# Spreading a looped front over gather columns by TensorE columns moved instead of by step count

## The chip, the cores and the metric

One core of one Trainium2 chip runs the whole program. The metric is the device time of one execution in microseconds (us), median of the timed runs. The profile describes one profiled execution.

## The reference, cut to what matters

One layer of a hybrid trunk over 512 prompt tokens, 16 meta tokens and 32 sample tokens with a cache of 256. Mixers first, then PEER, a retrieval over 128 x 128 single-neuron experts:

```python
h = _rms(x, ln1_g)
cq, ckv, kpe, bq, bk, bv, iq, iw, ik, ga, gb = split(h @ w_in)
o_a = softmax(q . k + mask) @ v                      # MLA, 8 heads
sel = top_k(sum_h iw * relu(iq . ik), k_sel)         # index of mixer B
o_b = softmax(bq . bk[sel]) @ bv[sel]                # 8 heads
x = x + (sigmoid(ga) * (o_a @ w_o_a) + sigmoid(gb) * (o_b @ w_o_b)) @ w_out
t = _rms(x, ln2_g)
e, g = product_keys(t @ peer_wq, subkeys)            # 8 heads x 16 experts of each token
a = gelu(einsum('td,thkd->thk', t, u[e]))
x = x + einsum('thk,thkd->td', g * a, v[e])
```

Each token reads 128 rows of u and of v (1,024 floats each), so the kernel gathers 544 x 128 x 8 KB from HBM.

## The kernel before, in words

**Two kinds of work in one stream.** After a first stage (`project`) and a first front, the kernel (`stream`) walks through 544 *columns* b. A block is 32 queries and has SG = 32 columns; a column is one indirect gather of 128 rows of 8 KB (1.05 MB) issued by GpSimd into one of RING = 9 buffers `rows` (L1191). For each column VectorE makes the dot products with u (`dot`, L2349) and, every second column, the arguments of the gelu; ScalarE makes weights and a diagonal (`diagonals`, L1901 to L1910); TensorE applies v with eight small matmul instructions (`mix`, L1600), three columns later (LAG = 3). A gather into a buffer waits until `mix` has read it nine columns before.

**Fronts.** A front is everything ahead of the gathers for one prompt tile of 128 tokens: row projection with `w_row` (L1214), norms and rotations, 24 attention units of 2 ticks each (8 index, 8 MLA, 8 DSA), gates (L1420), `w_o` (L1435), `w_out` (L1449), `peer_wq` (L1470), key scores. Front p (p = 1, 2, 3) runs inside columns 128(p-1) to 128p-1. It is written as a generator `front(p)` for each of TensorE, ScalarE and VectorE; each `yield` is a *tick*, of which a looped front has 117, and each engine's program calls `next(ahead)` `ticks_at(b)` times in column b. So `ticks_at` alone sets, on all three engines in the same way, in which column each step stands. All engines run in order: a step that waits holds back the columns behind it.

**Ticks.** They are numbered k = -32 to 84. For k < 0 the code uses x = k + 28: x = 2 sum of squares of the new rows (L1951), x = 4 scale, x = 5 transposes, x = 7 to 13 projection (two 512 KB chunks of `w_row` a tick, 416 KB at 13), x = 10 and 12 latent sums and norm (L1974, L1983), x = 16 the up-projections with `w_uq` and `w_ukv`, x = 18 to 25 norms, gains and rotations on VectorE, x = 23 and 26 transposes of pairs and heads. From k = 0 a unit starts at every even k: scores on TensorE at k, `index_unit` at k + 2 or `logits` at k + 1 on VectorE, probabilities, transposes and values up to k + 6. The eight MLA units (k = 17 to 31 on VectorE) also carry `choose_some`: two rounds of max and replace over the score row, for the top 128 of mixer B. Gates stand at two of every six ticks of k = 0 to 47; turn 54, mix 56 to 63, out 65 to 68, norm 69 to 72, ask 73 to 80, key scores 82 and 83.

**Not moved by ticks.** In each block VectorE also selects the experts of the next block (`choose`, 11 parts at columns 2, 4, ... 22 of the block), and a `spread` of the next rows stands in column 31 of a block (L1580). SyncE loads weights in program order into a ring of WRING = 4 chunks (L1113), each as soon as its slot's last user on TensorE is done. The new rows `xb` are loaded (L1124) behind `pe` work of the same stream:

```python
def load_x(i):
    if i >= 2:
        sp.wait_ge(s_xc, first_block(i - 1))
```

`s_xc` counts `residual`, which TensorE runs at column 3 of a block, so the rows for fronts 2 and 3 are asked for at column 3 of the window of 128 columns in which they are used.

Of the kernel before, what the change touches and what calls it, by code (L numbers as in the profile page):

```python
# [10 lines left out]

# [12 lines left out]
P = 128  # L27
D = 1024
DC = D // P
SEQ, DEC, META, PAST = 512, 32, 16, 256  # L30
# [11 lines left out]
H = 8  # L42
# [24 lines left out]
PH = 8  # L67
TOPE = 16
SLOTS = PH * TOPE
# [616 lines left out]
U = 2  # L686
# [8 lines left out]
SETTLE = 4  # L695
START = SETTLE + 28
# [33 lines left out]
        self.base = START if p else 0  # L730


def ticks_at(b):

    p = b // SLOTS + 1
    if p >= NP:
        return 0
    n, k = Ticks(p).all + Ticks(p).base, b % SLOTS
    done = lambda k: n * min(k, SLOTS - 4) // (SLOTS - 4)
    return done(k + 1) - done(k)  # L740


# [80 lines left out]
def stream(nc, io, m, sem):  # L823
# [187 lines left out]
    with psum("ps_h", [P, D]) as ps_h, psum("ps_v", [P, QD]) as ps_v, \  # L1011
# [183 lines left out]
        def _(pe):  # L1195
# [411 lines left out]
            for b in range(NCOL + LAG):  # L1607
                if b % SLOTS == 0 and b // SLOTS + 1 < NP:
                    ahead = front(b // SLOTS + 1)
                if b >= LAG:  # L1610
                    if (b - LAG) % SG == 0:
                        residual((b - LAG) // SG)
                    mix(b - LAG)
                if b < NCOL:
                    for _ in range(ticks_at(b)):
                        next(ahead)
                    n = b // SG
                    if b % SG == SG - 1 and n + 1 < NB:
                        spread(n + 1)

        @block.scalar
        def _(act):
# [306 lines left out]
            for b in range(NCOL + LAG):  # L1929
                if b % SLOTS == 0 and b // SLOTS + 1 < NP:  # L1930
                    ahead = front(b // SLOTS + 1)
                if b >= SG and b % SG == LAG - 1:
                    block_out(b // SG - 1)
                if 2 <= b <= NCOL and b % 2 == 0:
                    diagonals(b - 2)
                if b < NCOL:
                    n = b // SG
                    for _ in range(ticks_at(b)):
                        next(ahead)
                    if n + 1 < NB and b % SG == 17:  # L1940
                        softmax(n + 1)

        @block.vector
        def _(dve):
# [428 lines left out]
            for b in range(NCOL + 1):  # L2373
                if b % SLOTS == 0 and b // SLOTS + 1 < NP:
                    ahead = front(b // SLOTS + 1)
                n, k = b // SG, b % SG
                if b < NCOL and k:
                    dot(b)
                if b >= 2 and b % 2 == 0:
                    arguments(b - 2)  # L2380
                if b < NCOL:
                    for _ in range(ticks_at(b)):
                        next(ahead)
                    if k == 0:
                        dot(b)
                    if n + 1 < NB and k % 2 == 0 and 1 <= k // 2 <= PARTS:
                        choose(n + 1, k // 2 - 1)
# [138 lines left out]
```

## Time and profile before

| | |
|---|---|
| device time, median of 3 runs | 1838.06 us (1835.85 to 1842.35) |
| span of the profiled execution | 1831.0 us |
| busy: PE, PEld, DVE, ACT, POOL | 69%, 38%, 71%, 32%, 29% |
| bytes moved | 696.47 MB, of them 570.53 MB by the gathers |
| windows of 128 columns, by their first dot product | 238.2, 628.6, 1026.6, 1428.2, 1748.7 us |

The trace gives the span from the first to the last instruction, and no other time of its own for that execution; the median of the runs is 7.1 us above this span. PE is TensorE's matmuls, PEld its weight loads, DVE VectorE, ACT ScalarE, POOL GpSimd, SP SyncE. Column c is the c-th L2349 instruction of the trace, counted from 0.

### The profile page before, as it was taken

What the parts mean: (1) busy time and instruction counts of PE and PEld (TensorE: products, weight loads), DVE (VectorE), ACT (ScalarE), POOL (GpSimd) and SP (SyncE); (2) the same over time, 40 slices, a digit from 0 to 9 for tenths busy, and PEclk for the clock granted to TensorE, in tenths of its full rate; (3) what the DMA queues carried; (4) which work ended last, traced back from release to release, by engine and by line L of the source; (5) the groups of instructions that cost most, each with busy time, mean ns of one, the idle gap of its engine ahead of it and who ended that gap; (6) DMA issues with size and microseconds to landing.
All of it is one profiled execution on the core that took longest, in us unless ns stands there. A gap on an engine that the chain in (4) does not pass through costs nothing.

```text
span 1831.0 us, 26290 instructions
## 1 busy us (share of the span) xinstructions
PE 1256.7 (69%) x8990; PEld 693.1 (38%) x8990; DVE 1307.8 (71%) x3842; ACT 580.0 (32%) x2009; POOL 522.6 (29%) x569
## 2 busy tenths in 40 slices
PE   8989746678778565788877485889878543434353
PEld 3666612344444222455445132556536111111111
DVE  5561495888766577898767667898757768686754
ACT  2331223424323233334422333334423222222222
POOL 0100032333322323332323322322323333333332
PEclk9999859778798778788898587887997555555555
DMA  6325499999999999999999999998999999999997
GB/s 263 94 99 174 149 426 408 403 425 425 421 424 421 422 421 401 396 425 398 424 423 421 425 382 404 424 413 330 421 423 419 425 427 426 426 426 426 426 422 306
DMA packets 119380, 696.47 MB, mean 380 GB/s; under 512 B 17983, under 2 KB 21118, under 8 KB 49102
## 3 DMA queue, kind: packets, MB, share of 16 engines
q0 software_dynamic: 78848, 570.53, 74.7%
q1 hardware_dynamic: 36686, 121.83, 17.6%
q10 hardware_dynamic: 3712, 2.43, 0.4%
q8 instruction: 71, 1.16, 0.2%
q14 instruction: 63, 0.52, 0.1%
HBM read 691.65 MB, written 3.02 MB: 379 GB/s over the span
## 4 chain that ended last, share of the span: by engine, by line
DMA 37%; PE 27%; DVE 22%; issue 5%; ACT 4%; POOL 1%; ACTq 0%; DVEq 0%; POOLq 0%
DMA rows<-in_peer_uv,index 28%; DVE rows L2349 9%; PE ps_v L1600 6%; PE ps_f L1420 4%; PE ps_f L1470 3%; PE ps_f L1449 3%; DMA wch<-in_w_row 3%; PE ps_f L1214 3%; DMA wch<-in_w_out 2%; PE ps_h L1580 2%; DMA wch<-in_peer_wq 2%; PE ps_f L1435 1%; DVE score L2074 1%; DMA wch<-in_w_ukv 1%; PE ps_f L1298 1%
## 5 line engine op out<-in xcount | busy, mean ns | idle before, releaser
L1191 POOL DMA_INDIRECT rows<-in_peer_uv,index x544 | 512.7, 943 | 1211.4 <-PE ps_v L1600 1010.4
L2349 DVE CUSTOM_DVE_ANT_0 rows<-rows,ps_h 128x1024 f32<-128x1024 f32 x544 | 657.5, 1220 | 271.7 <-DMA rows<-in_peer_uv,index 228.7
L1600 PE MATMUL ps_v<-rows,diag 128*32 128x256 f32 x4352 | 434.2, 515 | 462.4 <-ACT diag L1910 462.1
L1600 PEld LDWEIGHTS ps_v<-rows,diag 128*32 128x32 f32 x4352 | 125.9, 133 | 719.2 <-ACT diag L1910 612.2
L1901 ACT ACTIVATE tan<-arg 128x2 f32<-128x2 f32 x272 | 55.4, 204 | 784.4 <-DVE arg L2359 765.4
L1904 ACT ACTIVATE weight<-tan,lead 128x1 f32<-128x1 f32 x544 | 180.8, 379 | 9.1
L1910 ACT ACTIVATE diag<-sel,weight 128x32 f32<-128x32 f32 x544 | 140.7, 305 | 0.0
L1420 PEld LDWEIGHTS ps_f<-bufh,wch 128*128 128x128 f32 x768 | 114.4, 233 | 22.0 <-issue 19.6
L1420 PE MATMUL ps_f<-bufh,wch 128*128 128x128 f32 x768 | 121.3, 323 | 0.0
L1214 PE MATMUL ps_f<-wch,bufh 128*128 128x512 f32 (+1 forms) x192 | 80.4, 559 | 18.3 <-DMA wch<-in_w_row 18.0
L1449 PE MATMUL ps_f<-wch,bufb 128*128 128x512 f32 x96 | 53.1, 693 | 18.4 <-DMA wch<-in_w_out 18.4
L1470 PE MATMUL ps_f<-bufh,wch 128*128 128x128 f32 x384 | 54.9, 302 | 10.8 <-DMA wch<-in_peer_wq 10.8
L1470 PEld LDWEIGHTS ps_f<-bufh,wch 128*128 128x128 f32 x384 | 50.4, 212 | 22.3 <-issue 16.5
L1214 PEld LDWEIGHTS ps_f<-wch,bufh 128*128 128x128 f32 x192 | 32.9, 202 | 60.6 <-issue 33.2
L1580 PE MATMUL ps_h<-hrows,rep 32*128 32x512 f32 x68 | 51.7, 898 | 3.0 <-DVE dots L2349 3.0
L2358 DVE TENSOR_TENSOR lead<-dots,halfw 128x2 f32<-128x2 f32 x272 | 43.9, 161 | 9.4
L1435 PE MATMUL ps_f<-bufq,wch 128*128 128x128 f32 x384 | 49.2, 281 | 0.8 <-DMA wch<-in_w_o 0.4
L1435 PEld LDWEIGHTS ps_f<-bufq,wch 128*128 128x128 f32 x384 | 44.7, 191 | 11.0 <-issue 9.2
L2349 DVE DVE_READ_ACCUMULATOR2_ANT dots<- 128x1 f32 x544 | 44.8, 82 | 0.0
L1715 ACT COPY probT<-ps_f 128x128 f32<-128x128 f32 (+3 forms) x64 | 26.5, 413 | 56.4 <-PE ps_f L1310 56.4
L2356 DVE SCALAR_TENSOR_TENSOR cube<-dots 128x2 f32<-128x2 f32 x272 | 42.7, 157 | 0.6
L2359 DVE SCALAR_TENSOR_TENSOR arg<-cube,dots 128x2 f32<-128x2 f32 x272 | 42.0, 154 | 0.0
(359 smaller groups left out, 1675.8 us busy)
## 6 DMA issues: line engine op xcount, KB each, us to landing
wch<-in_w_gate SPq DMA_DIRECT2D x60, 512.0 KB, 8.1
wch<-in_w_row SPq DMA_DIRECT2D x36, 512.0 KB, 11.3
wch<-in_w_o SPq DMA_DIRECT2D x32, 512.0 KB, 7.8
wch<-in_w_out SPq DMA_DIRECT2D x32, 512.0 KB, 10.1
wch<-in_peer_wq SPq DMA_DIRECT2D x32, 512.0 KB, 10.6
rows<-in_peer_uv,index POOLq DMA_INDIRECT x544, 13.8
w_tok<-in_w_tok SPq DMA_DIRECT2D x4, 1640.0 KB, 13.7
wch<-in_w_uq SPq DMA_DIRECT2D x6, 384.0 KB, 4.9
```

Of the source, the lines that this page charges most:

```text
L1191: pool.indirect_dma_start(rows[c % RING][:, :, :].rearrange("p a d -> p (a d)"), None, io.peer_uv[:, :], at).then_inc(s_uv[c % RING], 16)
L1214: ins = nc.tensor.matmul(ps_f[:, 2 + c % 2, 0:cols], buf_h[:, k, :], w[:, b, :], start=(k == 0), stop=(k == DC - 1))
L1420: ins = nc.tensor.matmul(gated(p)[:, a, :], w[:, k, :], h_of(p)[:, k, 0:n], start=(k == 0), stop=(k == DC - 1))
L1435: ins = nc.tensor.matmul(blended(p, j)[:, x, :], w[:, x, k, :], ot_of(p)[:, x, k, 0:n], start=(k == 0), stop=(k == 3))
L1449: ins = nc.tensor.matmul(ps_f[:, c, :], mt_of(p)[:, k, at_of(i)], w[:, 512 * c:512 * (c + 1)], start=(k == 0), stop=(k == DC - 1))
L1470: ins = nc.tensor.matmul(ps_f[:, 2 + n % 2, 0:x], w[:, k, :], h_of(p)[:, k, 0:x], start=(k == 0), stop=(k == DC - 1))
L1580: ins = nc.tensor.matmul(ps_h[:, 512 * j:512 * (j + 1)], rep[here, :, :].rearrange("p a m -> p (a m)"), hrows[i % 2][here, 512 * j:512 * ( ...
L1600: ins = nc.tensor.matmul(ps_v[GROUP * a:GROUP * (a + 1), :], diag[:, c % DRING, :], rows[c % RING][:, 1, QD * a:QD * (a + 1)], start=False ...
L1901: nc.scalar.activation(tan[:, s:s + 2], arg[:, s:s + 2], ACT.Tanh, scale=TANH).then_inc(s_tan, 1)
L1904: nc.scalar.activation(weight[:, s + j:s + j + 1], tan[:, s + j:s + j + 1], ACT.Identity, scale=lead[:, s + j:s + j + 1], bias=lead[:, s + ...
L1910: nc.scalar.activation(diag[:, (c + j) % DRING, :], sel[:, :], ACT.Copy, scale=weight[:, s + j:s + j + 1]).then_inc(s_diag, 1)
L2349: v.tensor_tensor_reduce(out=u, in0=u, in1=ps_h[:, :], scale=1.0, scalar=0.0, op0=ALU.mult, op1=ALU.add, accum_out=dots[:, c % KEEP:c % KE ...
```

## The change

`ticks_at` spreads the 117 ticks over the first 124 columns of the window. Before, tick t (0 to 116) stands where `117 * k // 124` passes it, so about one tick a column. After, each tick has a weight, the TensorE columns that it moves (`moved`), plus LIGHT = 320; ticks are cut at equal shares of the running sum. Nothing else changes: the same instructions, waits and loads on each engine, in the same order within each front and within each engine's column work.

```diff
+def moved(p):
+    at, nk = Ticks(p), META + P * p + P
+    tile_blocks = p + 1
+    due = lambda k, lag, low: k >= lag and (k - lag) % U == 0 and low <= (k - lag) // U < at.units
+    cols = []
+    for k in range(-at.base, at.all):
+        x = k + START - SETTLE
+        n = 0
+        if k < 0:
+            n += {5: 8 * 160, 8: 7 * 160, 13: 3 * 160, 16: 8 * 320, 23: 9 * 160, 26: 16 * 160}.get(x, 0)
+            if 7 <= x < 14:
+                n += 4 * 512 if x < 13 else 8 * 160
+            n = max(n, {2: 720, 4: 720, 6: 700, 10: 700, 12: 800, 16: 900, 18: 900, 19: 700, 21: 1000, 22: 1200, 23: 900,
+                        24: 900, 25: 600}.get(x, 0))
+        if due(k, 0, 0):
+            n += nk
+        if due(k, 3, H):
+            n += (tile_blocks + 1) * 160
+        if due(k, 5, H):
+            n += tile_blocks * 160
+        if 0 <= k < 6 * DC and k % 6 in (2, 4):
+            n += 8 * 160
+        if k == at.turn or k == at.rows or k == at.res:
+            n += 8 * 160
+        if at.mix <= k < at.mix + DC or at.ask <= k < at.ask + PH:
+            n += 8 * 160
+        if at.out <= k < at.out + 4:
+            n += 4 * 512
+        if k in (at.key, at.key + 1):
+            n += 8 * 160
+        cols.append(n + LIGHT)
+    return cols
+
+LIGHT = 320
+
 def ticks_at(b):
-    p = b // SLOTS + 1
+    p, k = b // SLOTS + 1, b % SLOTS
     if p >= NP:
         return 0
-    n, k = Ticks(p).all + Ticks(p).base, b % SLOTS
-    done = lambda k: n * min(k, SLOTS - 4) // (SLOTS - 4)
+    cols = moved(p)
+    ends = list(itertools.accumulate(cols))
+    done = lambda k: sum(e * (SLOTS - 4) <= ends[-1] * min(k, SLOTS - 4) for e in ends)
     return done(k + 1) - done(k)
```

## Rows read from the trace of the kernel before

**Rows 1.** The page: GB/s moved in 40 equal slices of the span

```profile
GB/s 263 94 99 174 149 426 408 403 425 425 421 424 421 422 421 401 396 425 398 424 423 421 425 382 404 424 413 330 421 423 419 425 427 426 426 426 426 426 422 306
```

**Rows 2.** Busy time by stretch: fronts 1, 2, 3 and the window without front

```profile
core 0: us, PE busy (x) PEld busy (x) DVE busy (x) ACT busy (x) POOL busy (x), PEclk, DMA share, GB/s
225.50:628.60 403.10, 281.26 (x2037) 156.28 (x2040) 304.63 (x921) 134.63 (x466) 126.70 (x134) 0.80 1.01 417
628.60:1026.60 398.00, 289.57 (x2108) 160.44 (x2109) 301.82 (x876) 138.12 (x464) 121.28 (x128) 0.83 1.01 415
1026.60:1428.20 401.60, 311.12 (x2204) 182.68 (x2208) 309.45 (x876) 142.63 (x464) 120.57 (x128) 0.81 0.99 404
1428.20:1748.70 320.50, 141.78 (x1076) 43.26 (x1080) 240.12 (x708) 84.62 (x328) 119.83 (x128) 0.51 1.01 426
```

**Rows 3.** The same view, shorter stretches in which GB/s falls

```profile
281.00:341.20 60.20, 37.77 (x210) 15.86 (x212) 38.76 (x100) 20.89 (x62) 16.06 (x17) 0.77 1.01 412
341.20:374.60 33.40, 25.77 (x207) 15.82 (x207) 29.39 (x93) 11.90 (x41) 12.74 (x14) 0.85 0.99 397
675.50:735.50 60.00, 36.66 (x211) 15.05 (x213) 38.61 (x100) 20.89 (x62) 16.24 (x17) 0.84 1.00 404
735.50:773.20 37.70, 30.97 (x231) 17.70 (x230) 33.81 (x106) 14.48 (x48) 14.38 (x15) 0.80 0.98 390
839.10:881.20 42.10, 38.53 (x279) 23.96 (x278) 36.92 (x121) 19.39 (x73) 13.26 (x14) 0.87 1.00 395
1074.40:1134.40 60.00, 37.27 (x200) 15.56 (x203) 38.71 (x100) 20.90 (x62) 15.12 (x16) 0.79 0.98 391
1134.40:1174.30 39.90, 34.56 (x252) 21.19 (x252) 36.49 (x109) 15.12 (x48) 15.22 (x17) 0.80 0.98 400
1174.30:1228.20 53.90, 43.22 (x290) 29.14 (x294) 49.88 (x127) 18.80 (x67) 15.18 (x16) 0.81 1.01 419
1228.20:1280.90 52.70, 48.90 (x329) 33.03 (x327) 44.39 (x131) 20.44 (x72) 14.06 (x15) 0.81 0.88 339
```

**Rows 4.** Waits, 1060 to 1135 us: total, times, longest

```profile
ACT sg L1633 <- PE ps_f L1214: 19.3, 3, 13.0
...
DVE pst L1983 <- ACT pst L1644: 9.3, 1, 9.3
...
DVE rel L1999 <- ACT oab L1656: 5.4, 1, 5.4
```

**Rows 5.** TensorE in order of time during the third front's projection

```profile
1061.29 3.70 PE L1214 MATMUL ps_f<-wch,bufh 128*128 128x512 f32 x8
...
1074.16 1.98 PE L1214 MATMUL ps_f<-wch,bufh 128*128 128x512 f32 x4 [1.17 <-DMA wch<-in_w_row]
1079.20 3.78 PE L1214 MATMUL ps_f<-wch,bufh 128*128 128x512 f32 x4 [3.06 <-DMA wch<-in_w_row]
```

**Rows 6.** VectorE in order of time, column 310 to 312

```profile
1187.33 0.70 DVE L2094 CUSTOM_DVE_ANT_0 logit<-ps_f,biasA 128x528 f32<-128x528 f32 x1
...
1191.05 0.69 DVE L2298 TENSOR_TENSOR cand<-posf,num 128x512 f32<-128x512 f32 x1
...
1193.23 1.22 DVE L2349 CUSTOM_DVE_ANT_0 rows<-rows,ps_h 128x1024 f32<-128x1024 f32 x1
...
1195.85 0.19 DVE L2303 SCALAR_TENSOR_TENSOR index<-pick 128x32 uint32<-128x32 f32 x1
```

**Rows 7.** The page's DMA issues: count, KB, median us to landing

```profile
wch<-in_w_row SPq DMA_DIRECT2D x36, 512.0 KB, 11.3
...
rows<-in_peer_uv,index POOLq DMA_INDIRECT x544, 13.8
```

**Rows 8.** The new rows of front 2: issue on SP

```profile
632.44 0.33 SPq L1124 DMA_DIRECT2D xb<-in_x_prompt  x1
```

**Rows 9.** VectorE around it: columns 130 and the first sum

```profile
630.86 1.22 DVE L2349 CUSTOM_DVE_ANT_0 rows<-rows,ps_h 128x1024 f32<-128x1024 f32 x1
...
647.37 1.22 DVE L1951 CUSTOM_DVE_ANT_0 oab<-xb 128x1024 f32<-128x1024 f32 x1
```

**Rows 10.** The view of tile xb: issue to landing

```profile
DMA to landing us min/median/max: 7.2/8.3/8.7
```

More of the change, by code:

```diff
@@ L15 @@
+import itertools
 import numpy as np
```

## The prediction

> **What bounds the kernel now.** I read the slices first. From the sixth slice on the DMA engines move 419 to 427 GB/s, except in a few slices at 330 to 413 [rows 1]: the loop over gather columns is bound by DMA, and what is left to gain are the dips. The window without a front takes 320.5 us for 128 columns, 2.50 us a column, at 426 GB/s with VectorE 75% and TensorE 44% busy [rows 2]. So a faster engine is worth nothing as such; time is won only where the transfers run dry.
>
> How much is that? Stretches with a front that do not dip run at 419 to 425 GB/s [rows 1, 3]; I take 421 as their ceiling, my choice. Idle time is then stretch x (1 - GB/s / 421): 403.1 us at 417 gives 3.8 us, 398.0 at 415 gives 5.7, 401.6 at 404 gives 16.2 [rows 2], in all 25.7 us. This is the most that any spreading of the steps can win.
>
> The shorter stretches say where [rows 3]. *Projection and heads*, x = 7 to 27 (columns 18 to about 45 of a window): 1.3 + 1.9 us in front 1, 2.4 + 2.8 in front 2, 4.3 + 2.0 in front 3, together 14.7. *Attention*: 2.6 us in front 2 (839 to 881), 10.3 in front 3 (1228 to 1281: 52.7 x 82/421), together 12.9. The two sums make 27.6, two more than the windows, since other stretches lie above 421.
>
> The waits tell why the first kind dips. In front 3 ScalarE waits up to 13.0 us for the second projection group, VectorE behind it 9.3 us for the root of the latents (L1983), and later 5.4 us for the up-projection [rows 4]. Behind VectorE stand the dot products, behind those `mix`, behind that the gathers. The cause is the load: a 512 KB chunk lands 11.3 us after its issue [rows 7], its slot is freed two ticks before it is needed, and before the change two ticks are two columns, some 5 us.
>
> The second kind is work. A unit with `choose_some` in front 3 takes VectorE 3.72 us (1187.33 to 1191.05), a column with its arguments 1.31 us (1193.23 to 1195.85, two columns), a part 8 or 9 of `choose` 2.18 us (1191.05 to 1193.23) [rows 6]. From 1193.23 (column 311) to 1228.2 (column 320) nine columns take 35.0 us [rows 3, 6], where DMA needs 9 x 2.50 plus two gate chunks at 1.25 (0.524 MB at 421 GB/s), 25.0 us. The gathers absorbed about 10 us of lag before GB/s fell: that is the slack of the ring, and I use it below.
>
> **The change, part by part.** It removes and adds no instruction. I worked out the new columns from `moved`: the weights sum to 142,768, 150,960 and 159,152, thus 1,151 to 1,283 a column.
>
> *Projection* (x = 7 to 13, weight 2,368 each, 3,488 at 8) stood in columns 12 to 19. It now stands in 8 to 21 (front 1), 7 to 19, 7 to 18: 1.8 to 2.1 columns a tick. SP's chunk loads move with their users. From freeing to need there are now four columns at 2.50 us plus four chunks at 1.25 us, 15 us, against 11.3 us to landing [rows 7]. The waits of 9.3 and 5.4 us go [rows 4]. From column 18 to 32 VectorE is busy 38.7 of 60 us [rows 3]; with the 9.3 and 5.4 us of waits gone it needs 45, and DMA needs 14 x 2.50 plus some eight chunks, 45. So DMA should hardly idle. Short waits stay: the up-projection (x = 16) and its copy (x = 17) fall into one column in all three fronts, and norms of 1 to 3 us follow densely. I leave 1.4 us of idle for each front: 14.7 - 4.2 = 10.5 us won. Bounds: 0 (the waits return elsewhere) and 14.7.
>
> *Index units and choose_some* (k = 0 to 31) stood in columns 34 to 67. They stand in 32 to 63 in front 3, and not evenly: k = 0 to 18 shrinks from 20 columns to 14. `moved` counts TensorE's columns, not VectorE's work. The heavy units k = 17 to 31 move from columns 52 to 67 to 45 to 63; before, they began as `choose` ended (columns 34 to 54), now they share 45 to 54 with its parts 6 to 10. A part costs 1.65 us in the mean: without a front VectorE is busy 240.1 us, 128 x 1.31 of them for columns, 72 for 44 parts [rows 2, 6]. VectorE in columns 45 to 63: 19 x 1.31 + 8 x 3.72 + 5 x 1.65 + 2 (final selection and last index unit, three passes over the score row, each like L2094's 0.70 [rows 6]) = 65 us. DMA: 19 x 2.50 + 5 gate chunks = 53.7. Lag grows by 11.5 us. With up to 3 us brought along and 10 of slack, 1.5 to 4.5 us are lost; if the slack is only 7, up to 7.5.
>
> *Units k = 28 to 47* stood in 20 columns of front 3 (64 to 84) and get 24 (60 to 84). TensorE is busy 48.9 of 52.7 us there [rows 3], and its work per column falls by a sixth, to about 2.5 to 2.9 us, DMA's own pace. The tail of the dip goes. So front 3's attention loses 6 us after against 10.3, a gain of 4.3 (bounds: 10.3, and a loss of 4 if there is no slack at all). In front 2 rows of 400 keys cost less; 2.6 becomes 1.5, a gain of 1.1. Front 1 has no dip there and gets none.
>
> *The new rows.* Empty ticks x = -4 to 1 took columns 1 to 6; x = 2 stood in column 7 and now stands in column 2. VectorE finishes column 130 at about 632.3, and the load of `xb` is issued at 632.44 [rows 8, 9], 15 us ahead of its use at 647.37 before. It lands after 8.3 us [rows 10], so VectorE now stands still until about 641, in fronts 2 and 3. Behind it stand the dot products from column 131, ScalarE at its root, and `mix` from column 130; up to seven issued gathers, 17 us of transfers, are outstanding. The first gather that waits for the late `mix` follows at about 649, before they end. I charge 1 us a front, 2 in all (bounds 0 and 4 each).
>
> *Ticks that now share a column* (for instance k = 51 to 53, where TensorE needs ScalarE's copy and VectorE the result) wait for each other at close range. VectorE is under 60% loaded there, so the ring hides most; 2 us, bounds 0 and 6. The steps from 56 on move by at most seven columns, in stretches at 419 to 425 GB/s [rows 1]: nothing.
>
> Sum: -10.5 - 4.3 - 1.1 + 2 + 2 = -11.9 us. The profiled span of 1831.0 becomes 1819.1; the median of the runs, 7.1 us above the span, becomes 1826.2.
>
> **A rule against it.** In the rows a chunk after a wait of 1.17 us runs in 1.98 us, after one of 3.06 us in 3.78 us, at the lower clock level [rows 5]. Spreading leaves more gaps, but each holds a `mix`: of 6.8 us per projection tick TensorE works about 5. The Trainium skill (TensorE: Matmul & The Clock Gate, Loop structure matters more than you think) asks for matmuls back to back, and calls a long DMA wait between them the bad case, since the array goes cold. By that the sum would be the third rival's; by the row with the short wait it is mine.
>
> **Rivals.** *Idle time only moves* (0.22). Front 3's overload of VectorE comes ten columns earlier, and what the projection wins is lost in columns 40 to 63 and at column 2. For it: the same 310 us of VectorE work [rows 2]. Against it: the waits of 9.3 and 5.4 us are not work [rows 4]. Time: -5 to +5, about 1838.
>
> *Pile-up on VectorE: slower* (0.10). The slack is spent at column 40 by the heads. Then lag turns into idle time in full: 14.5 us in front 3 (+4 against 10.3), about 7 in front 2 (+4.5), 4 in front 1 (+4), and the projection wins only half, 5: with +2 and +2, about +11, 1849. It decides when more than some 8 of 10 us of slack are gone at column 40. Against it: after the heads the ring refilled, since GB/s is back at 419 from 1174 [rows 3].
>
> *A cold projection: slower* (0.08). At 3.78 us a chunk, 12.8 chunks, 13 columns of `mix` at 1.08 and 1.8 for the gains take TensorE 64 us against 48.5 for DMA: 15.5 less 10 of slack is 5.5 us lost a front, over 4.9 now. Instead of winning 10.5 it costs 2: +0.6, and +5 if half of the slack is used, 1843. It decides above about 3.3 us a chunk.
>
> The forecast, a gain of more than 0.3%, has 0.58; 0.02 is left for other losses.
>
> **Numbers.** A difference under 0.3% (5.5 us) can't be told from none. Faster 0.58, same 0.22, slower 0.20. The low end is 1816: nearly 22 of the 25.7 us. The high end, 1844, takes in the moved idle time and the cold projection and part of the pile-up. The forecast's own range is 1816 to 1832.
>
> **What would show it.** Right: no 9 us wait of L1983 on L1644; 415 GB/s or more through projection and heads; the third window under 396 us. A new wait of L1951 for the load of `xb` of 7 to 9 us in fronts 2 and 3. VectorE above 95% busy from column 45 to 63 of front 3, with the dip there, earlier and shallower. Wrong: that dip deeper than 10 us, GB/s falling near column 10 of windows 2 and 3, or L1214 chunks mostly at 3.7 us.

## The result: 0.64% slower

The changed kernel takes 1846.98 us in the median of 6 runs (1845.93 to 1850.64), the kernel before 1836.95 us in 6 runs (1830.6 to 1842.35). The ratio is 1.0064, with a 95% interval of 1.0043 to 1.0085, so it is slower by 12 us (the two medians are 10.0 us apart) where the forecast was 12 us faster. The profiled span went from 1831.0 to 1844.1 us.

First the slices of the page after, against [rows 1]: the GB/s moved.

```profile
GB/s 261 95 98 173 155 425 422 417 425 424 425 424 422 422 349 423 421 387 398 425 423 422 392 400 395 412 331 366 424 422 424 426 426 426 425 426 424 427 420 304
```

Some dips are gone (408 and 403 in slices 7 and 8, 401 and 396 in slices 16 and 17 [rows 1]), and new ones stand beside them (349 in slice 15, 392 to 400 in slices 23 to 25), while the deepest has doubled its width (331, 366). Busy time by stretch, for the three windows with a front and the one without, against [rows 2]:

```profile
core 0: us, PE busy (x) PEld busy (x) DVE busy (x) ACT busy (x) POOL busy (x), PEclk, DMA share, GB/s
225.50:628.10 402.60, 285.04 (x2039) 159.94 (x2041) 305.73 (x922) 135.65 (x467) 127.21 (x134) 0.79 1.01 420
628.10:1030.30 402.20, 292.21 (x2109) 164.93 (x2112) 301.45 (x876) 137.94 (x464) 121.26 (x128) 0.82 0.99 407
1030.30:1441.40 411.10, 305.19 (x2204) 181.79 (x2208) 309.56 (x876) 142.24 (x464) 121.37 (x128) 0.81 0.98 396
1441.40:1762.00 320.60, 141.32 (x1076) 43.32 (x1080) 240.13 (x709) 84.61 (x328) 119.82 (x128) 0.51 1.01 426
```

The engines' busy times are those of before to within three per cent, and the last window is the same to 0.1 us. The difference is time in which DMA has nothing to move. By the prediction's measure, stretch x (1 - GB/s / 421), this idle time is 1.0, 13.4 and 24.4 us in the three windows, against 3.8, 5.7 and 16.2: front 1 wins 2.8, front 2 loses 7.7, front 3 loses 8.2, together 13.1 us, the 13 us of the span. Only the sum is firm: the windows themselves got 0.5 us shorter, 4.2 and 9.5 us longer, since a gather can be moved early, in the window ahead of its column. Shorter stretches of fronts 2 and 3 say where. They are cut at columns 0, 18 and 32, and for front 3 also at 45, 64 and 88:

```profile
628.10:683.90 55.80, 34.95 (x203) 14.62 (x202) 40.09 (x129) 18.38 (x52) 16.07 (x17) 0.75 0.91 360
683.90:736.40 52.50, 30.64 (x180) 13.55 (x184) 38.68 (x101) 17.51 (x57) 14.52 (x15) 0.75 1.02 423
1030.30:1086.90 56.60, 35.52 (x194) 14.57 (x194) 40.67 (x131) 18.51 (x52) 15.06 (x16) 0.72 0.95 379
1086.90:1143.30 56.40, 32.89 (x204) 15.20 (x208) 37.84 (x97) 19.76 (x61) 15.38 (x16) 0.76 1.02 422
1143.30:1176.60 33.30, 28.45 (x215) 18.88 (x216) 31.09 (x92) 12.96 (x41) 11.69 (x12) 0.87 0.96 386
1176.60:1246.10 69.50, 51.12 (x365) 32.96 (x363) 63.61 (x161) 21.20 (x75) 18.95 (x21) 0.79 0.92 354
1246.10:1314.00 67.90, 58.48 (x433) 39.81 (x433) 54.38 (x165) 28.83 (x102) 22.49 (x24) 0.85 0.97 384
```

Three things are to be seen. Columns 18 to 32, at 404 and 391 GB/s before [rows 3], are full at 423 and 422. Columns 0 to 18, full before (424 and 425 GB/s), are at 360 and 379: 8.1 and 5.6 us idle. And columns 45 to 64 of front 3 take 69.5 us at 354 GB/s, 11.1 us idle.

The waits in 1060 to 1145 us, against [rows 4]:

```profile
ACT sg L1674 <- PE ps_f L1255: 15.4, 3, 6.5
...
DVE rel L2040 <- ACT oab L1697: 6.9, 1, 6.9
```

ScalarE's longest wait for a projection group fell from 13.0 to 6.5 us, and VectorE's 9.3 us for the root of the latents (L1983 on L1644) is gone. The wait for the up-projection (L1999 on L1656 before) is still there, and grew from 5.4 to 6.9 us.

**Columns 0 to 18.** The waits in 626 to 665 us (total, times, longest):

```profile
PE ps_f L1241 <- DVE qh L2001: 10.3, 1, 10.3
DVE oab L1992 <- DMA xb<-in_x_prompt: 8.4, 1, 8.4
```

L1992 is L1951 of before, the sum of squares of the new rows. It waits 8.4 us for the load, as forecast. What follows in GpSimd's, TensorE's and DMA's time is in these rows, first the gather issues:

```profile
636.48 0.94 POOL L1232 DMA_INDIRECT rows<-in_peer_uv,index  x1 [0.30 <-issue]
649.76 0.94 POOL L1232 DMA_INDIRECT rows<-in_peer_uv,index  x1 [12.35 <-PE ps_v L1641]
655.28 0.94 POOL L1232 DMA_INDIRECT rows<-in_peer_uv,index  x1 [3.35 <-PE ps_v L1641]
661.68 1.09 POOL L1232 DMA_INDIRECT rows<-in_peer_uv,index  x1 [5.46 <-PE ps_v L1641]
```

then TensorE's first projection tick,

```profile
654.91 5.89 PE L1255 MATMUL ps_f<-wch,bufh 128*128 128x512 f32 x8
```

and busy time in steps of 4 us:

```profile
644.00:648.00 4.00, 1.97 (x8) 1.57 (x8) 3.86 (x14) 0.75 (x3) 0.00 (x0) 0.50 0.73 309
648.00:652.00 4.00, 1.93 (x16) 0.59 (x16) 3.90 (x9) 0.54 (x3) 1.87 (x2) 0.50 0.27 57
652.00:656.00 4.00, 2.10 (x10) 0.77 (x11) 3.83 (x16) 1.29 (x5) 0.71 (x1) 0.50 0.90 360
656.00:660.00 4.00, 4.00 (x7) 1.67 (x6) 3.83 (x16) 1.29 (x5) 0.22 (x1) 0.58 0.99 372
660.00:664.00 4.00, 4.00 (x31) 1.55 (x30) 3.93 (x9) 1.29 (x5) 2.02 (x2) 1.00 0.88 288
664.00:668.00 4.00, 4.00 (x27) 2.48 (x29) 3.83 (x14) 1.76 (x6) 0.95 (x2) 1.00 0.89 323
```

The next gather is issued at 649.76; the prediction said "about 649". But the transfers under way ended at about 647, not after 649, so DMA stands almost still from 648 to 652 (57 GB/s). Then VectorE is busy 3.8 of every 4 us and TensorE, at the low clock level (0.50), needs 5.89 us for two chunks. The ring has little in reserve, so a second dip follows from 660 to 668: at 656 us 1.5 gathers are issued and not yet moved, at 662 us 1.0. (This is counted from the trace: the gathers that GpSimd has issued, less what their queue has moved at 1.049 MB each.)

The low level isn't new, though. In the kernel before, the first projection tick of this front and a step of 4 us ahead of it read:

```profile
659.01 5.24 PE L1214 MATMUL ps_f<-wch,bufh 128*128 128x512 f32 x8
```

```profile
656.00:660.00 4.00, 3.22 (x19) 1.10 (x18) 3.96 (x6) 1.22 (x5) 1.22 (x2) 0.50 1.02 432
```

There too the granted clock is 0.50 and the tick is slow, and DMA stays full at 432 GB/s. What differs is the reserve when it comes: 3.4 gathers issued and not yet moved at 656 us, and not 1.5.

### The profile page after: what moved, and what is told of

Its sections match the earlier page's. It is cut to its first block, busy times and chain, and to the rows that moved or that the text cites. A ratio compares the mean times of both kernels' runs of the same rounds, so it can differ in the third digit from the quotient of the medians.

```text
span 1844.1 us, 26278 instructions
## 1 busy us (share of the span) xinstructions
PE 1255.8 (68%) x8990; PEld 700.4 (38%) x8990; DVE 1308.2 (71%) x3842; ACT 579.9 (31%) x2009; POOL 523.8 (28%) x569
## 4 chain that ended last, share of the span: by engine, by line
DMA 34%; PE 27%; DVE 24%; issue 5%; ACT 3%; POOL 1%; ACTq 1%; DVEq 0%; POOLq 0%
DMA rows<-in_peer_uv,index 26%; DVE rows L2390 9%; PE ps_v L1641 6%; DMA wch<-in_w_row 4%; PE ps_f L1461 3%; PE ps_f L1476 3%; PE ps_f L1490 2%; PE ps_h L1621 2%; PE ps_f L1511 2%; PE ps_f L1255 2%; DVE score L2115 2%; DVE best L2114 2%; DMA wch<-in_w_out 1%; POOL rows L1232 1%; ACT diag L1951 1%
## 5 line engine op out<-in xcount | busy, mean ns | idle before, releaser
L1641 PE MATMUL ps_v<-rows,diag 128*32 128x256 f32 x4352 | 426.7, 509 | 458.1 <-ACT diag L1951 457.7
L1951 ACT ACTIVATE diag<-sel,weight 128x32 f32<-128x32 f32 x544 | 141.1, 306 | 1.8 <-PE ps_v L1641 1.7
L1476 PE MATMUL ps_f<-bufq,wch 128*128 128x128 f32 x384 | 58.0, 313 | 0.9 <-ACT bufq L1805 0.9
L1476 PEld LDWEIGHTS ps_f<-bufq,wch 128*128 128x128 f32 x384 | 53.1, 222 | 12.4 <-issue 8.2
L1339 PE MATMUL ps_f<-bik,bufb 64*128 64x144 f32 (+2 forms) x96 | 38.5, 488 | 1.7 <-ACT kt L1726 1.0
## 6 DMA issues: line engine op xcount, KB each, us to landing
wch<-in_peer_wq SPq DMA_DIRECT2D x32, 512.0 KB, 10.1
```

Of the source, the lines that this page charges most:

```text
L1476: ins = nc.tensor.matmul(blended(p, j)[:, x, :], w[:, x, k, :], ot_of(p)[:, x, k, 0:n], start=(k == 0), stop=(k == 3))
L1641: ins = nc.tensor.matmul(ps_v[GROUP * a:GROUP * (a + 1), :], diag[:, c % DRING, :], rows[c % RING][:, 1, QD * a:QD * (a + 1)], start=False ...
L1951: nc.scalar.activation(diag[:, (c + j) % DRING, :], sel[:, :], ACT.Copy, scale=weight[:, s + j:s + j + 1]).then_inc(s_diag, 1)
```

## The experiments

Each is the kernel before or after with another column for some ticks, but for the two that leave work out. A ratio is to the kernel before in the same rounds and is known to about 0.2%, so a difference of two ratios is known to some 0.25 to 0.3%, about 5 us. `was(p, t)` is the column of tick t before, `now(p, t)` after, `START` = 32 is the tick k = 0. Theory A has two separate prices, the early wait for the rows and VectorE's overload in the attention, and a gain from the projection. B puts all of the loss in the attention, C all in the early wait.

**Only the first nine ticks early.**

```diff
+def column(p, t):
+    return now(p, t) if t < 9 else was(p, t)
```

> The kernel before, with only the first nine ticks of each looped front (x = -4 to 4: four ticks' worth of nothing, the sum of squares of the new rows, its root, the scaling) in the columns in which the change puts them, x = 2 in column 2 instead of 7. Everything from x = 5 on stands as before. Theory A (the early wait for the new rows runs the ring dry): 6 to 13 us slower than before, a wait of 8 to 9 us of the sum of squares for the load of xb in fronts 2 and 3, GB/s well under 400 in the 20 us behind it. Theory B (the loss is the pile-up of VectorE work in the attention, and the ring absorbs the early wait): under 2 us slower, GB/s over 410 there.

Measured: 1846.74 us, ratio 1.0055 (1.0033 to 1.0077), 10 us slower. Waits in front 2, and columns 0 to 18 of both fronts:

```profile
DVE oab L2013 <- DMA xb<-in_x_prompt: 7.8, 1, 7.8
```

```profile
628.00:677.00 49.00, 26.60 (x171) 11.13 (x170) 39.67 (x127) 15.03 (x47) 14.05 (x15) 0.69 0.96 391
1034.00:1083.20 49.20, 27.08 (x172) 11.38 (x169) 39.63 (x127) 15.03 (x47) 14.04 (x15) 0.69 0.97 395
```

Nine ticks with about 2 us of VectorE's work cost nearly as much as the whole change. B, in which the ring absorbs the wait, is out. The wait is 7.8 us, a little under the 8 to 9 expected. Only 6.5 us of idle time stand at the spot; with the projection still in column 12, the second dip of the change is missing. The rest is spread over later stretches of this profile (384 GB/s in columns 64 to 88 of front 2, 344 in front 3), where lag meets dips that are there anyway. How it divides between places in other runs, one profile can't say.

**TensorE's transposes early too.** The same with `t < 10`.

> As the run with only ticks x = -4 to 4 early, and in addition x = 5, TensorE's transposes of the scaled rows, in column 5 or 4 as in the change, so that TensorE too waits for the late rows and holds back its mix instructions. If TensorE's wait adds to the price: 3 to 8 us slower than that run, 13 to 18 slower than before. If VectorE's wait is all of it (my expectation, as mix for column 130 can't run earlier in any case): within 3 us of that run.

Measured: 1845.76 us, 1.0043 (1.0023 to 1.0062). By this run the early rows cost 8 us. No more than the run above: TensorE's wait of 9.3 us adds nothing measurable to VectorE's.

**Only the attention moved.**

```diff
+def column(p, t):
+    return max(now(p, t), 33) if START <= t < START + 54 else was(p, t)
```

> The kernel before, with only ticks k = 0 to 53 (index, MLA and DSA units and gates) in the columns in which the change puts them; k = 17 in column 49, 47, 45 instead of 52. Projection, heads and everything from k = 54 on stand as before. Theory A (both places cost): 4 to 9 us slower than before, of it 1 to 3 in front 2 and 3 to 6 in front 3, the dip of front 3 beginning some seven columns earlier. Theory B (all of the loss is here): 10 to 14 us slower. Theory C (the deeper dip in the attention is only lag brought along from the early wait): within 2 us of before.

Measured: 1849.49 us, 1.0054 (1.0033 to 1.0075), some 10 us slower, a little above what A gave it and at the lower end of B's. Columns 48 to 64 and 64 to 88 of front 3:

```profile
1194.40:1248.20 53.80, 41.62 (x294) 27.80 (x294) 49.60 (x125) 18.83 (x67) 14.23 (x16) 0.81 0.87 323
1248.20:1316.30 68.10, 58.70 (x433) 39.70 (x433) 54.48 (x167) 28.93 (x102) 22.77 (x24) 0.85 0.97 384
```

53.8 x 98/421 = 12.5 us idle, as in the change, though there was no wait for new rows. C is out: the dip is made on the spot. Front 2 of this profile lost more than A's 1 to 3 us: 12.5 us idle over its window, against 5.7 before.

**The change without its attention.**

```diff
+def column(p, t):
+    return now(p, t) if t < START else max(was(p, t), now(p, START - 1))
```

> Ticks x = -4 to 27 as in the change (new rows in column 2, projection spread over 7 to 21), everything from k = 0 on in the columns of before. So the change without its attention. The early rows alone cost about 10 us, the attention alone about 10, the whole change about 10; if these add up, spreading the projection wins about 10, and this kernel is within 3 us of before, idle time in columns 0 to 18 as in the change (8.1 and 5.6 us in fronts 2 and 3), none in 18 to 32. If the spread projection wins nothing: 8 to 12 us slower than before.

Measured: 1840.85 us, 1.0032 (1.0018 to 1.0046). 6 us slower, outside the 3 I gave, and short of the 8 to 12 for no gain at all. Against the run with nine early ticks (1.0055) the projection's gain is 4 us, against the one with ten (1.0043), which moves x = 5 as this one does, 2 us, and neither is clear of the noise of a difference. Idle time is 7.3 and 4.3 us in columns 0 to 18, and -0.2 and 0.8 in 18 to 32.

**The rows late again.** Empty ticks weigh more, so x = 2 stands in column 6 or 7 and k = 17 in 52, 50, 48.

```diff
-        cols.append(n + LIGHT)
+        cols.append(n + (1280 if x < 2 else LIGHT))
```

> The changed kernel with a weight of 1,280 instead of 320 for the six empty ticks, so that x = 2 stands in column 6 or 7 again; the projection still has 11 to 13 columns (11 to 25), and k = 17 stands in column 52, 50, 48. Theory A: no wait of L1992 for xb above 1 us; 9 to 15 us faster than the changed kernel, so 0 to 5 us faster than before. Theory B: 0 to 3 us faster than the changed kernel, so 7 to 10 us slower than before.

> x_late once more beside the two others and the kernel before on the same chip, to place the projection's gain in the same rounds: between the change with its rows late and the hand-fitted run. Spread projection and late rows with the change's own attention: 2 to 6 us faster than before.

Measured twice: 1834.54 us, 0.9977 (0.996 to 0.9994), and 1833.44 us, 0.998 (0.9965 to 0.9995). No wait for `xb` is left in either profile. Against the changed kernel's ratio of 1.0064 this is 0.85% or 16 us, a little more than the 9 to 15 expected. One constant turns the change from a loss into a small gain. Not all of it is the wait, since the heavy units moved by three columns too.

**Late rows and equal attention.** In addition to the edit above:

```diff
+    a = at.base
+    cols[a:a + at.turn] = [sum(cols[a:a + at.turn]) // at.turn] * at.turn
```

> As x_late, and in addition ticks k = 0 to 53 share their columns equally, so that k = 17 stands in column 53 or 54 and k = 31 in 67, as before. Left of the change are the spread projection and the last third. Theory A: 8 to 14 us faster than before; the dips of the attention as before or smaller, those of projection and heads gone. Theory C: the same as x_late within 2 us. If the spread projection won nothing: within 2 us of before.

Measured: 1832.86 us, 0.9975 (0.9953 to 0.9998), 1828 to 1841 in 12 runs. A had asked for 8 to 14 us, and got 4.5. The time is the one that C gave, the same as with the rows late alone (0.9975 against 0.9977), though C itself was out already. Columns 48 to 64 of front 3 are nearly full (1.2 us idle), but 64 to 88 lose 16.7 us in the profiled execution. That one took 1840.89 us and belongs to four of the twelve at 1840 to 1841; the other eight took 1828 to 1835, and none of them was profiled. Equal spacing gives TensorE's dense units back the few columns of before. In this one profile the dip moved on.

**The rounds left out,** in both kernels:

```diff
             def choose_some(i, h):
                 q, nk = queries(i), keys(i)
+                if i >= 2:
+                    return
```

> The changed kernel without the max and replace rounds of choose_some in the looped fronts (the top 128 of mixer B isn't selected there), 3 us of VectorE work less in each of eight units a front; all else stays. If the idle time in columns 48 to 64 (3.6 us in front 2, 11.1 in front 3) is VectorE's overload: it falls to under 1 us in both, and the kernel is 10 to 18 us faster than the changed one, so 0 to 8 us faster than before; what stays is the early wait for the rows. If it is something else that moved with the ticks (TensorE, waits between engines that now share a column): less than 5 us faster than the changed kernel.

> The kernel before without the same rounds. If the idle time in columns 64 to 88 of front 3 (10.6 us) is lag that the rounds in columns 52 to 67 leave behind: it falls to under 4 us, and the kernel is 7 to 12 us faster than before. If it is TensorE's own density there (48.9 of 52.7 us busy): it stays above 6 us, and the kernel is under 5 us faster.

Measured: 1826.84 us after, 0.9944 (0.9925 to 0.9964), and 1825.17 us before, 0.9925 (0.9899 to 0.9951). Columns 45 to 64 of front 3 after:

```profile
1171.30:1227.70 56.40, 49.29 (x364) 32.87 (x367) 40.42 (x113) 24.04 (x84) 18.79 (x20) 0.86 1.01 425
```

With 23 us of VectorE work fewer (40.4 against 63.6) the stretch is full, at the same spacing and the same TensorE work: the idle time there was VectorE's. Taking the work away wins 1.2% or 22 us after, where 10 to 18 were expected, and 14 us before, where 7 to 12 were. The two kernels no longer differ measurably. In before, the idle time of columns 64 to 88 falls from 10.6 to 3.9 us: most of that dip, which I had in part laid to TensorE, was lag from the rounds.

**A placement by hand for both engines.** On top of x_late:

```python
def column(p, t):
    at = Ticks(p)
    k, c = t - at.base, now(p, t)
    for lo, hi, a, b in ((0, 16, now(p, at.base), 51), (17, 31, 52, 66), (32, 47, 67, 88), (48, 53, 89, 90)):
        if lo <= k <= hi:
            c = a + (b - a) * (k - lo) // (hi - lo)
    return c if k < 54 else max(c, 90)
```

> As x_late (rows late, projection spread), but with the attention fitted to both engines by hand: index units one tick a column up to column 51, the heavy units k = 17 to 31 in 52 to 66 between two choose sweeps of VectorE, and k = 32 to 47, TensorE's dense part, over 67 to 88 instead of 66 to 84 or so. If places of both engines decide: idle time of columns 48 to 88 of front 3 under 8 us, 2 to 6 us faster than x_late, so 6 to 11 faster than before. If the dip of 64 to 88 comes whatever the spacing: within 2 us of x_late.

> The hand-fitted run once more, beside fit_att and x_late on the same chip: 10 to 15 us faster than before, and by the projection's gain faster than fit_att.

Measured: 1824.25 us, 0.9927 (0.9904 to 0.995), and in other rounds 1828.14 us, 0.9955 (0.994 to 0.997): 8 to 13 us faster than before, the best of all with the full work done. The first was a little better than the 6 to 11 us expected, the second missed the low end of its 10 to 15. Front 3, columns 0 to 18, 18 to 32, 48 to 64, 64 to 88:

```profile
1027.90:1075.30 47.40, 31.43 (x198) 13.03 (x198) 40.06 (x129) 15.04 (x48) 15.42 (x16) 0.68 1.01 425
1075.30:1132.50 57.20, 34.14 (x188) 14.38 (x188) 38.56 (x100) 20.89 (x61) 15.64 (x16) 0.86 1.02 421
...
1172.10:1228.70 56.60, 45.74 (x323) 31.97 (x324) 53.49 (x134) 21.13 (x73) 15.98 (x17) 0.85 1.00 408
1228.70:1295.10 66.40, 59.95 (x446) 39.66 (x445) 58.26 (x172) 27.73 (x96) 22.00 (x24) 0.85 0.94 368
```

Idle 1.7 + 8.4 = 10.1 us in columns 48 to 88, not under 8, and hardly less than the 10.9 of before; what front 3 wins stands in columns 18 to 32 (4.3 us before, none here).

**The same attention with the old projection.** `was(p, t)` in place of `now(p, t)`, k = 0 in column 34, and the steps from k = 54 on in the columns of before.

> Projection and heads as before, ticks k = 0 to 53 as in the hand-fitted run. It splits that run's gain of 13 us. If most of it is the spread projection: 0 to 6 us faster than before, with idle time in columns 18 to 32 as before (1.3, 2.4, 4.3 us). If most of it is the attention: 8 to 13 us faster than before.

Measured: 1832.57 us, 0.9988 (0.9968 to 1.0008), so 0 to 6 us faster as for "mostly the projection", with 1.7, 2.9 and 2.7 us idle in columns 18 to 32. In the same rounds the hand placement is at 0.9955: spreading the projection, with the rows late, is worth 0.33%, 6 us, give or take 5. The two also differ in the steps from k = 54 on, by a few columns.

Idle us in fronts 2 / 3, from one profile of each of seven kernels, by the measure above (slightly negative where GB/s is above 421), cut at these columns:

| | 0-18 | 18-32 | 32-48 | 48-64 | 64-88 |
|---|---|---|---|---|---|
| before | -0.4 / -0.5 | 2.4 / 4.3 | 2.6 / 2.0 | -0.5 / 0.3 | 2.4 / 10.6 |
| after | 8.1 / 5.6 | -0.2 / -0.1 | 0.0 / 2.7 | 3.6 / 11.1 | 2.2 / 6.0 |
| rows early | 3.5 / 3.0 | 1.2 / 1.0 | 4.8 / 4.4 | -0.5 / 0.3 | 6.5 / 13.3 |
| attention only | -0.3 / -0.5 | 2.6 / 2.7 | 4.5 / 1.5 | 1.3 / 12.5 | 5.5 / 6.0 |
| x_late | 0.0 / -0.4 | -0.3 / 0.0 | 2.9 / 1.3 | 2.4 / 6.8 | 4.5 / 3.7 |
| after, no rounds | 7.8 / 6.0 | -0.2 / 0.3 | -0.3 / 4.0 | -0.4 / -0.4 | -0.2 / 0.5 |
| fit | -0.3 / -0.5 | -0.3 / 0.0 | 1.0 / 1.2 | -0.2 / 1.7 | 5.7 / 8.4 |

## Why the prediction was wrong

The frame held: the loop is bound by DMA, the windows' idle time accounts for the difference of the spans, and each of the places named moved. Two terms had the wrong size, and with them the sum the wrong sign. By the table, fronts 2 and 3 win 8.9 us in columns 18 to 48 and lose 14.6 in 0 to 18 and 10.1 in 48 to 88; front 1 wins 2.8.

- **The new rows** were charged 2 us. The wait (8.4 and 8.9 us) and the time of the next gather (649.76) were forecast nearly to the microsecond. The failing step is "I charge 1 us a front". It rested on "up to seven issued gathers, 17 us of transfers". Counted as above, 3.3 gathers were issued and not yet moved at 632.3 us, and two more were issued before the pause: 5.3 gathers, 13 us at 2.50 each, and they ended 2 to 3 us before the next gather. The charge also left out that the projection now stands right behind, where the emptied queue of gathers is hit again, and it took a spent reserve to be free. Measured alone: 8 to 10 us.
- **The attention** was to win 5.4 us and costs 10 alone. The failing step is "With up to 3 us brought along and 10 of slack, 1.5 to 4.5 us are lost". VectorE's 65 us of work were right (63.6 measured), but the stretch took 69.5 us, as VectorE also waited 6, and lag beyond DMA's 53.7 was 16, not 11.5. Of it only some 5 were absorbed (11.1 idle). The slack of 10 isn't a constant, it is what stands issued when the lag begins. By the same count the nine columns from 1193.23 in before began with 4.5 gathers outstanding and ended with 1.0; after, the stretch began with 2.3 (column 45) and 1.9 (column 48). The gain expected in columns 64 to 88 came (10.6 to 6.0), since they got more columns, but is the smaller part.
- **The projection** was to win 10.5 us, and here the mechanism is right: the 9.3 us wait is gone, and columns 18 to 32 are full. The 5.4 us wait, said to go, became 6.9, without idle time at the spot. In the one profile the idle time of columns 18 to 48 fell about as forecast (8.9 us in fronts 2 and 3). By time the gain is smaller, 2 to 4 us with the rows early and 6 with them late, each give or take 5. So part of what the dips cost seems to come back later; that is not shown apart from the noise.
- **Small readings.** Of the 14.7 us laid to projection and heads 6.7 stood in columns 32 to 45, where x = 27 is over at 33 and the index units run. Columns 18 to 32 were to need 45 us and took 52.5 and 56.4 in fronts 2 and 3, at full pace, as DMA moved 16 to 18 gathers there and not 14. The 2 us for ticks that share a column didn't come (425 GB/s or more in columns 82 to 88 after), and columns 88 to 128 stayed full, as said. The 7.1 us between span and median compare two executions: each run is 1.8 to 1.9 us above its own span, so the profiled execution before took some 1833 us, 5 below its median.
- **The signs.** The waits for `xb` came as written, and the 9 us wait went. VectorE was 92% busy in columns 45 to 64, not above 95%, the third window took 411 us and not under 396, and two signs of being wrong came: the dip deeper than 10 us, and GB/s falling near column 10.
- **The rivals.** The pile-up on VectorE (0.10, 1849 us) was nearest, but it came near by another path: its condition, slack spent by the heads at column 40, isn't what happened. At column 40 of front 3 there were 4.3 gathers outstanding after, 2.5 before; VectorE was overloaded enough by itself. "Idle time only moves" (0.22) named both places of loss. The cold projection did not come as a state: columns 18 to 32 ran at 423 and 422 GB/s. (Its "+5 if half of the slack is used" would be 5 in each of three fronts, 15.)

What stays open: why the early rows cost 8 to 10 us when 6.5 are idle at the spot, and how much of the projection's gain lasts. The parts (rows and projection as in the change, 0.32%, and attention, 0.54%) sum to 0.86% against 0.64% for the whole; with intervals of 0.14% to 0.21% to each side that is no contradiction.

## What to carry to other kernels

A weight that decides where work stands must be that of the engine that is short there: here TensorE's columns placed work that VectorE had to do, on top of the expert selection, which the weight didn't know. Before moving an "empty" step earlier, follow what its first real instruction waits for back to the event that permits the load; here five columns of about 2.5 us had covered a transfer of 8.3 us. And a ring's reserve is not a constant: count the gathers that stand issued where the lag begins, 4.5 at one place here and about 2 at another.

## What the runs showed of the hardware

Ahead of the projection of front 2 the granted clock stood at 0.50 in both kernels, in after with a wait of 10.3 us in it, in before with TensorE busy 3.2 of 4 us or less. The first two chunks of 128x512 matmuls took 5.89 us after and 5.24 before, 5.97 against 4.65 in front 3, and 5.88 against 4.24 in front 1; the second tick, once the clock was at 1.00, took 3.70 us in both kernels. So the change added 0.6 to 1.6 us to this tick of each front, and no cold projection: after, each later full chunk took 1.95 to 1.98 us or a pair 3.70, with waits of up to 1.75 us between them. In before one wait of 3.06 us had been followed by a chunk at 3.78 us [rows 5]; with the steps spread it didn't recur.

A load of the new rows (512 KB) landed 7.7 to 9.0 us after its issue in the change, and 7.2 to 8.7 before [rows 10], with 3 to 4 gathers' worth of transfers ahead of it in front 2.
